# The two layers of the second block written out, with two heads' query and key tiles ahead of the values, other places for the taps, and an end that keeps only squares

## The reference, cut to what matters

```python
for l in range(2):
    h = rmsnorm(x, mix_norm_g[l])
    u = h @ w_in[l]               # a_b, a_c, a_x | q, k, v | c_in
    y_a = a_b * conv3(a_c * a_x)                        # causal, depthwise, 3 taps
    q, k = rope(q), rope(k)                             # 4 heads, 2 maps of 64 each
    p = softmax(mask(q @ k.T / 8))                      # for both maps
    o = (p[0] - lam * p[1]) @ v;  y_b = rmsnorm(o, g) * (1 - lam_init)
    c = (c_in + b)[:256] * sigmoid((c_in + b)[256:])
    y_c = silu(layernorm(conv31(c) + b))                # causal, depthwise, 31 taps
    x = x + concat(y_a, y_b, y_c) @ w_out[l]
    h = rmsnorm(x, ffn_norm_g[l])
    x = x + (silu(h @ w_gate[l]) * (h @ w_up[l])) @ w_down[l]
return rmsnorm(x, final_norm_g)
```

## Time and profile before

| | us |
|---|---|
| median of 3 runs | 1922.26 (1921.88 to 1922.32) |
| the profiled execution, its own time | 1923.04 |
| its span, first to last instruction | 1921.2 |
| PE busy in the span | 1874.6 |
| PE idle in the span | 46.6 |
| mean granted clock | 0.993 |

### The profile page before, as it was taken

One profiled execution on the slowest core, in us unless ns is written; L12 is line 12 of the kernel. 1 busy time (PEld: TensorE's weight loads), 2 busy tenths in 40 slices (PEclk: granted clock), 3 DMA queues, 4 the chain that ended last, 5 costly groups with the idle time before them and its releaser, 6 DMA issues.

```text
span 1921.2 us, 29986 instructions
## 1 busy us (share of the span) xinstructions
PE 1874.6 (98%) x8654; PEld 1505.5 (78%) x8654; DVE 852.5 (44%) x1316; ACT 739.2 (38%) x1172; POOL 1111.7 (58%) x1318
## 2 busy tenths in 40 slices
PE   7999999999999999989999999999989999999996
PEld 6876668888888888767888888887767888888885
DVE  7677643455555122766433232121766442323213
ACT  5245553432323223566433322222556432223222
POOL 4442236567766665855556566665865555665664
PEclk9999999999999999999999999999999999999998
DMA  7111112222222332321232222332321222222232
GB/s 249 66 55 45 49 51 99 99 88 98 98 98 99 107 100 99 105 69 59 88 99 98 97 89 98 107 101 101 100 74 60 87 94 97 94 98 98 99 109 87
DMA packets 52036, 178.14 MB, mean 93 GB/s; under 512 B 6512, under 2 KB 7664, under 8 KB 51696
## 3 DMA queue, kind: packets, MB, share of 16 engines
q1 hardware_dynamic: 51952, 177.09, 27.7%
HBM read 169.76 MB, written 2.10 MB: 89 GB/s over the span
## 4 chain that ended last, share of the span: by engine, by line
PE 84%; DVE 4%; issue 2%; POOLq 2%; ACT 2%; POOL 1%; DVEq 1%; DMA 1%; SPq 1%; ACTq 0%
PE bank L536 22%; PE bank L516 21%; PE bank L517 21%; PE bank L573 3%; PE bank L574 3%; PE bank L580 3%; POOLq L477 2%; POOL wl L459 1%; DMA turned<-ybuf 1%; PE bank L773 1%; PE bank L819 1%; PE bank L805 1%; PE bank L556 1%; SPq L429 1%; PE bank L550 1%
## 5 line engine op out<-in xcount | busy, mean ns | idle before, releaser
L459 POOL TENSOR_TENSOR wl<-raw,wh (+1 forms) x1252 | 1029.6, 854 | 737.0 <-ACT wh L1002 737.0
L1002 ACT ACTIVATE wh<-raw 128x1024 fp32r (+1 forms) x313 | 331.8, 1060 | 833.0 <-PE bank L536 692.9
L516 PE MATMUL bank<-xh,wh 128*128 128x512 f32 x1336 | 525.9, 394 | 0.0
L517 PE MATMUL bank<-xl,wh 128*128 128x512 f32 x1336 | 522.6, 391 | 0.0
L536 PE MATMUL bank<-xh,wl 128*128 128x512 f32 x1336 | 340.5, 394 | 0.0
L536 PEld LDWEIGHTS bank<-xh,wl 128*128 128x128 f32 x1336 | 249.7, 189 | 61.6 <-issue 11.1
L516 PEld LDWEIGHTS bank<-xh,wh 128*128 128x128 f32 x1336 | 252.2, 189 | 58.3 <-issue 5.0
L517 PEld LDWEIGHTS bank<-xl,wh 128*128 128x128 f32 x1336 | 252.3, 189 | 51.9
L516 PE MATMUL bank<-hh,wh 128*128 128x512 f32 x528 | 205.4, 389 | 0.0
L517 PE MATMUL bank<-hl,wh 128*128 128x512 f32 x528 | 205.4, 389 | 0.0
L1416 DVE TENSOR_TENSOR ybuf<-bank,rstd 128x512 f32<-128x512 f32 x95 | 65.3, 689 | 239.7 <-PE bank L536 237.6
(11 more groups left out here) (292 smaller groups left out, 2201.5 us busy)
## 6 DMA issues: line engine op xcount, KB each, us to landing
raw<-in_weights SPq DMA_DIRECT2D x313, 512.0 KB, 3.2
turned<-ybuf SPq DMA_DIRECT2D x64, 64.0 KB, 2.0
xs<-in_x SPq DMA_DIRECT2D x4, 512.0 KB, 7.3
out_t<-xs SPq DMA_DIRECT2D x8, 256.0 KB, 2.0
w1k<-in_w SPq DMA_DIRECT2D x1, 1024.0 KB, 9.4
w1v<-in_w SPq DMA_DIRECT2D x1, 1024.0 KB, 10.2
shifted<-kvraw SPq DMA_DIRECT2D x8, 124.0 KB, 2.4
posi<-in_positions SPq DMA_DIRECT2D x2, 256.0 KB, 8.4
```

The source lines that it names most:

```text
L459: x_ = pool.tensor_tensor(wl[:, :, :].rearrange("p s n -> p (s n)")[:, two], raw[:, cols((v % 4) * (CB * P) + h * part, part)], wh[:, :, : ...
L516: mm(b[:, :], w, kh(k), start=first and k == 0, stop=False)
L517: mm(b[:, :], w, kl(k), start=False, stop=False)
L1002: return act.activation(o, i, ACT.Copy, scale=scale)
```

## The change

In each layer the q and k tiles of heads 0 and 1 (four chunks) move ahead of the values; the slots of the heads stay at 22. So `vgroup` is now chunks 8 to 11, and the head steps 0 and 1 of head 0 fall into its last chunk. Its banks are others (`VB`), and their four tiles are taken out by ACT (two, in slot 22) and DVE (two, at the end of chunk 11) in place of ACT alone. The 31 taps on DVE go to chunks 5 to 14 in place of 4 to 8, and ACT copies their result in slot 29 in place of 18. SP puts the swap of chunk n ahead of the load of chunk n + 5. The layers' loop is written out on all four engines. In the last `down` nothing is written to xh and xl, the last tile's square goes to PE by itself, a root of a zero stands ahead of the last wait on ACT, the last products read the bank, and the two chunks beyond the end are gone.

```diff
-POOL_TAPS = {6: 3, 7: 2, 8: 2, 9: 2, 10: 3, 11: 3, 12: 3, 13: 3, 14: 2, 15: 2, 16: 2, 17: 2, 18: 2}
+POOL_TAPS = {6: 1, 7: 1, 8: 1, 9: 1, 10: 1, 11: 2, 12: 3, 13: 3, 14: 3, 15: 4, 16: 4, 17: 4, 18: 3}
+def qk_tile(n):
+    return n - 4 if 4 <= n < 8 else n - 8 if 12 <= n < 16 else None
-        VB = [G[0], G[1], ROT, POOLB]
-        QK0 = [TR, OUT]
+        VB = [G[N_BLOCK1 % 2], OUT, ROT, G[1 - N_BLOCK1 % 2]]
...
@@ SP: loads and swaps
-                loads(done, T + 14)
+                loads(done, T + 9)
                 for i in range(8):
+                    if i == 4:
+                        for t in range(T + 13, T + 17):
+                            load(t, t)
+                    t = T + (9 if i < 4 else 13) + i
                     turn_halves(l, i)
-                    load(T + 14 + i, T + 14 + i)
+                    load(t, t)
...
@@ POOL, PE, ACT, DVE alike
-            with pool.Fori(0, LAYERS) as l:
+            for l in range(LAYERS):
...
@@ PE: a layer
                 def turn_l(h, i):
+                    if h == 0 and i == 0:
+                        pe.wait_ge(R["v_out"], Count(2).loop(l, 2).value())
...
-                vgroup(T + 4, N, {(1, 0): lam_sum})
-                for m in range(4, N_LIN):
+                for m in range(4, 8):
+                    xk(T + m, N + m, slots=[lambda: slot(m, 0), lambda: slot(m, 1)], lag=5 if m < 6 else 1)
+                vgroup(T + 8, N, {(c, half): lambda c=c, half=half: slot(8 + c, half)
+                                  for c in range(4) for half in range(2)})
+                for m in range(8, N_LIN):
                     n = m + 4
-                    if m == 6:
-                        pe.wait_ge(R["v_out"], Count(NT).loop(l, NT).value())
+                    if m < 10:
+                        pe.wait_ge(R[("v_out", "v_rest")[m - 8]], Count(1).loop(l, 2).value())
...
@@ PE: the end
-            x_stats(Count(U_BLOCK1 + LAYERS * U_LAYER), Count((2 + 2 * LAYERS) * KD))
+            pe.wait_ge(xl_ready, (2 + 2 * LAYERS) * KD + KD - 1)
+            mm(STAT[:, 0:NT], ident, zero4, start=True, stop=True)
+            for i in range(NT):
+                mm(STAT[:, i:i + 1], sqacc[:, i * P:(i + 1) * P], one, start=False, stop=True, skip_group_check=True)
+            pe.wait_ge(R["last_sq"], 1)
+            for i in range(NT):
+                x_ = mm(STAT[:, i:i + 1], sq[:, (KD - 1) % 2, i * P:(i + 1) * P], one, start=False, stop=True,
+                        skip_group_check=True)
+            x_.then_inc(stat_ready, 1)
...
@@ ACT: a layer, and the end (last_down)
+                        if s == 22:
+                            for i in range(2):
+                                act.wait_ge(R["v_psum"], Count(i + 1).loop(l, 2).value())
+                                copy(lv[:, :, i, :], VB[i][:, :].rearrange("p (h d) -> p h d", d=P),
+                                     scale=s_recip[:, i:i + 1]).then_inc(R["v_out"], 1)
-                        if s == 18:
+                        if s == 29:
                             act.wait_ge(R["conv_done"], L1.value())
...
+                act.activation(small[:, 190:191], zero, ACT.Sqrt)
+                act.wait_ge(tile_out, (n + 2).value())
+                act.activation(sq[:, (KD - 1) % 2, :], xs[:, KD - 1, :], ACT.Square).then_inc(R["last_sq"], 1)
...
@@ DVE: a layer, and the end
-                BANK_TAPS = {4: (0, 3), 5: (4, 4), 6: (4, 4), 7: (4, 4), 8: (2, 2)}
+                BANK_TAPS = {5: (1, 1), 6: (1, 1), 7: (1, 1), 8: (2, 2), 9: (2, 2), 10: (2, 2), 11: (1, 1), 12: (2, 2),
+                             13: (2, 2), 14: (3, 0)}
...
-                        if half == 1 and 9 <= n < 17:
-                            rot_end(n - 9)
+                        if half == 1 and qk_tile(n - 1) is not None:
+                            rot_end(qk_tile(n - 1))
...
+                    if n == 11:
+                        dve.wait_ge(chunk_done, (T + 12).value())
+                        for i in (3, 2):
+                            ts(lv[:, :, i, :], VB[i][:, :].rearrange("p (h d) -> p h d", d=P), s_recip[:, i:i + 1],
+                               None, ALU.mult).then_inc(R["v_rest"], 1)
...
-            x_norm(Count(U_BLOCK1 + LAYERS * U_LAYER))
+            recips(u, NT)
+            dve.wait_ge(bc_ready, (u + 1).value())
             for m in range(KD):
-                mul3(xs[:, m, :], xs[:, m, :], c2("next_g", m), rstd[:, :]).then_inc(R["out_ready"], 1)
+                mul3(xs[:, m, :], xs[:, m, :], c2("next_g", m), BC[:, :]).then_inc(R["out_ready"], 1)
```

More of the change, by code:

```diff
@@ L891, in _ @@
             down(tb, nb, Count(KF))
-            with pe.Fori(0, LAYERS) as l:
+            for l in range(LAYERS):
                 T = Count(T_BLOCK1).loop(l, T_LAYER)
@@ L1240, in down, with last_down @@
                     feed(r * 2 + 1, (feed0 + 1).loop(r, 2), gain("next_g", r * 2 + 1), (n + 1).loop(r, 2))
+            def last_down(t, n, feed0):
+                with act.Fori(0, KD // 2 - 1) as r:
+                    for c in range(2 * DOWN_CHUNKS):
+                        tt = (t + c).loop(r, 2 * DOWN_CHUNKS)
+                        act.wait_ge(chunk_done, (tt + 1).value())
+                        head(tt + 2)
+                        if c == DOWN_CHUNKS:
+                            feed(r * 2, feed0.loop(r, 2), None, n.loop(r, 2))
+                    feed(r * 2 + 1, (feed0 + 1).loop(r, 2), None, (n + 1).loop(r, 2))
+                t, n, feed0 = t + 6 * DOWN_CHUNKS, n + 6, feed0 + 6
+                for c in range(2 * DOWN_CHUNKS - 2):
+                    act.wait_ge(chunk_done, (t + (c + 1)).value())
+                    head(t + (c + 2))
+                    if c == DOWN_CHUNKS:
+                        feed(KD - 2, feed0, None, n)
+                act.activation(small[:, 190:191], zero, ACT.Sqrt)
+                act.wait_ge(tile_out, (n + 2).value())
+                act.wait_ge(xl_ready, feed0.value())
+                act.activation(sq[:, (KD - 1) % 2, :], xs[:, KD - 1, :], ACT.Square).then_inc(R["last_sq"], 1)
             def gain1(name, m):
@@ L1249, in _ @@
             down(t, n, Count(2 * KD), gain1)
-            with act.Fori(0, LAYERS) as l:
+            for l in range(LAYERS):
                 T = Count(T_BLOCK1).loop(l, T_LAYER)
@@ L1776, in down, with last_down @@
                 dve.drain()
+            def last_down(t, n, feed0):
+                for m in range(KD):
+                    add_to_x(t + (DOWN_CHUNKS * (m + 1) - 1), n + m, m)
+                    if m < KD - 1:
+                        dve.drain()
+                        feed(m, feed0 + m, None)
+                dve.drain()
             def gain1(name, m):
@@ L1785, in _ @@
             down(t, n, Count(2 * KD), gain1)
-            with dve.Fori(0, LAYERS) as l:
+            for l in range(LAYERS):
                 T = Count(T_BLOCK1).loop(l, T_LAYER)
```

71 lines of the change are left out of this document (38 added, 33 removed).

## The result

The changed kernel takes 1911.86 us, median of 4 runs (1911.20 to 1912.56), against 1922.29 us for the kernel before: 10.4 us less, ratio 0.9947 with a 95% interval of 0.9935 to 0.9959. The forecast was 1907.2 us, range 1900 to 1916. The sign and the range hold; the gain is two thirds of the 15.1 us in my sum, and it doesn't lie where I put it.

What follows compares the result with a forecast made beforehand. TensorE, busy 98%, bounds the kernel. Gains of 1.8 us (layers written out), 8.2 (24.8 of stalls and clock less 16.6 new) and 5.1 (the end) sum to 15.1, giving 1907.2 us, range 1900 to 1916.

Steps and rivals of the forecast that it cites:

- The layers written out: At the second layer's start, TensorE's 1.8 us wait, taken for the loop's jump back, goes; bounds 0 to 1.8.
- The key tile's wait and the value bank: Head 0's key tile wait, 2.7 us per layer, falls away; the first value tile's bank costs a new 0.6 us.
- The stalls in chunks 13 to 17: New TensorE stalls per layer: 0.8 us in slots 27 and 28, 2.7 in chunk 14, 3.3 in slots 31 to 34.
- The clock: Behind chunk 14's stall the clock may fall once for 3.4 us, costing 1.7; half counted, 0.9 per layer.
- POOL costed at nothing: Chunks 15 to 17 hold four POOL additions in place of two; costed at nothing, since POOL's split runs a chunk ahead.
- The swaps: Swaps issued ahead of loads, so four transfers start without a load in flight; counted 0, ends 0 and 1.5 us per layer.
- The end: After x's last tile, earlier square and sums and no copy to `rstd` gain 5.1 us, of 3.9 to 5.8.
- A: The prediction's own sum holds: about 1907 us, own range 1903 to 1912; chance 0.50.
- C: The waits only move: new stalls cost what old ones did; end and jump alone win 6.9 us: 1915.3; chance 0.19.
- E: GpSimd's additions and VectorE block each other, 7.4 us a layer, so no change: 1921.9 us; chance 0.06.
- B: DVE's taps are hidden, chunk 14 costs nothing, clock holds, about 3.5 us of stalls per layer: 1897.5 us; chance 0.18.
- one window at 0.50 per layer or none: Sign in the profile after: at most one stretch per layer with TensorE's granted clock at 0.50, that is 1.2 GHz.

Runs made afterwards that it cites:

- e4: The kernel before with only its four loops over the layers written out on PE, ACT, DVE and POOL; 1918.3 us.
- e3: The changed kernel with DVE's taps moved forward, more in chunks 8 to 10 and none in 13 and 14; 1911.4 us.
- e1: The changed kernel with POOL's table of additions per chunk as before the change, ACT's products moving with it; 1906.6 us.
- e2: The changed kernel with POOL's additions of taps 16 and later one column wide, output not the reference's; 1900.3 us.
- e5: The changed kernel with ACT's products for taps 16 and later one column wide, output not the reference's; 1902.1 us.
- e8: e3 with ACT's copy of the finished convolution in slot 26 in place of 29; 1908.8 us.
- e9: The changed kernel with SP again issuing a chunk's load ahead of the swap; 1911.7 us.
- e6: e8 with POOL's table of additions as before the change, as in e1; 1901.3 us.
- e12: e6 with one of POOL's additions moved from chunk 11 to chunk 14; 1898.9 us.
- e10: e6 with POOL's additions 3 in each of chunks 6 to 10 and 2 in each of 11 to 18; 1909.0 us.
- e11: The changed kernel without the root of a zero ahead of ACT's last wait; 1911.0 us in one run.

## Why the prediction was partly right

- **The layers written out**, forecast 1.8 us: 2.0 at the place named, right. Together with e4's second half it is 3.9, which I missed.
- **The key tile's wait and the value bank**: 2.7 us gone, and with it the waits for exponentials in slots 24 to 26. The value bank's wait is 0.2 us, where I took 0.6; another 0.4 us stands at the first chunk of the values, where I had nothing. That the two make 0.6 is chance.
- **The stalls in chunks 13 to 17**: forecast 0.8 + 2.7 + 3.3 us. Measured in the changed kernel: 0.4 in slot 27, 0.35 + 1.62 in slot 30, and 3.1 in slots 31 to 34. Then 1.8 us in slot 37, where I had nothing. In all 7.9 us against 7.4. The sum is near by luck, for the causes were not right: e3 shows that DVE's taps have little part in it, and e1, e2, e5 and e8 that POOL's additions, ACT's products and ACT's copy do.
- **The clock**, the step that failed: "Behind the stall of chunk 14 the clock may fall once, [...] and I count half, 0.9." It fell twice a layer, behind slots 33 and 37, and cost 3.4 us a layer. That is 5.0 of the 6.8 us between the 8.2 forecast for this part and the 1.4 measured. I had tied the clock to stalls of 2.7 us; here waits of 1.3 us, with a shorter one just ahead, came before it. The trace of before already had one such window, at 1413.2 us behind a wait of 1.5 us, and I passed over it. The other 1.8 us are the stalls' 0.9 for both layers and what lies within the spread of single profiles. Behind the stall of chunk 14 itself it did not fall.
- **POOL costed at nothing**, wrong: e1 puts its table at 5.2 us for both layers, together with ACT's products, which move with it. I asked only whether TensorE would wait for POOL; it doesn't. POOL's price is paid on DVE, and in slot 37 the trace shows it whole.
- **The swaps**, 0: right by e9.
- **The end**, 5.1 us: 5.75. The square begins 0.03 us behind the last addition, the sums 0.69 us behind the square's start, as worked out. The clock held for the sums and the spreading (1.05 and 0.65 us in place of 1.87 and 1.12), and reading the bank in the eight multiplications costs nothing: 5.36 against 5.39 us. I had taken 5.1 of a range of 3.9 to 5.8, less than all of this.
- **The rivals.** The time lies at the edge of A's own range. By mechanism it is C: end and jump are won, 7.7 us, and the waits of the attention have only moved, with 1.4 us left over. I gave C 0.19 and priced it 3.4 us too slow. And what moved them is in good part the mechanism of E, which I gave 0.06, at about a third of its price. B (taps hidden) is nearly true of DVE's taps themselves, by e3. With the taps, ACT's copy and POOL's additions all earlier (e6, e12) the time is 1901.3 and 1898.9, near B's 1897.5.
- **The signs**: of those that I named, "one window at 0.50 per layer or none" failed; there were two. "Gathered around slots 30 and 31" failed too: 2.9 of the 7.9 us of waits stand there. The waits in chunks 12 to 17 came to 5.5 us, between my bounds of 4 and 11.

## What to carry to other kernels

When work is moved on an engine that nobody waits for, look at what runs beside it at the new place: additions on POOL were free by the waits of TensorE, and their table cost 5 us, in part through DVE's instructions with two inputs in SBUF and in part through the products on ACT that move with them. When a change trades one set of short waits for another, count the clock's windows and not only the waits. And try a table of work per chunk one entry at a time: e12 differs from e6 by one addition and from e10 by three, and is 2.4 and 10 us faster.

## What the runs showed of the hardware

- A DVE instruction with two SBUF inputs that began just behind a POOL addition ended just behind it: 1.34 us in place of 0.35 (128x128). One of 128x512 took 1.70 in place of 0.70. Twelve of them in 44 us each ended 0.15 us (128x128), 0.28 us (128x256) or 0.55 us (128x512) behind the end of a POOL addition or split.
- The granted clock fell to 0.50 for 3.4 us behind single waits of 1.3 us, in the attention's short products. But not always behind the same ones. The changed kernel's 1.62 us wait at 842.44 had no window behind it, and in e11, with the same code there, a wait of 1.63 us at 842.65 had one. In e2 waits of 1.6 us had none in either layer, and in e5 one of 0.83 us, in layer 2, had one.
- With the layers' loops written out (e4), and so without their one jump back, layer 2's first product came 2.0 us earlier.
- The table of the square root took 1.28 us, and the activation began 0.01 us behind it.
